# Thirteen pairs of value pieces as 2x2 block products of seven instead of eight, in the second half of both value stages

## The reference, cut to what matters

```python
def block(args):
    ht, et, gt = args
    act = jax.nn.gelu(jnp.einsum('td,ted->te', ht, u[et]), approximate=False)
    return jnp.einsum('te,ted->td', gt * act, v[et])
```

## Time and profile before

| | us |
|---|---|
| median of three runs | 2201.44 (2199.56 to 2203.94) |
| span of the profiled execution | 2200.3 |
| TensorE busy | 2187.5 (99%) |
| VectorE busy | 1649.6 (75%) |
| ScalarE busy | 1223.3 (56%) |
| GpSimd busy | 719.4 (33%) |

### The profile page before, as it was taken

One profiled execution on the slowest core, in us unless ns is written; L12 is line 12 of the kernel. 1 busy time (PEld: TensorE's weight loads), 2 busy tenths in 40 slices (PEclk: granted clock), 3 DMA queues, 4 the chain that ended last, 5 costly groups with the idle time before them and its releaser, 6 DMA issues.

```text
span 2200.3 us, 43642 instructions
## 1 busy us (share of the span) xinstructions
PE 2187.5 (99%) x14230; PEld 1905.3 (87%) x14230; DVE 1649.6 (75%) x3276; ACT 1223.3 (56%) x1933; POOL 719.4 (33%) x737
## 2 busy tenths in 40 slices
PE   9999999999999999999999999999999999999999
PEld 8899888888888888888988888888888888899887
DVE  8776885888888755666678678888886556558895
ACT  6555555555544445565565555554444446566764
POOL 1506886333344100002088853324440001530000
PEclk9999999999999999999999999999999999999999
DMA  5265665555655566554556655555556665545665
GB/s 175 97 200 156 189 188 176 172 172 170 187 177 179 180 193 191 172 192 134 173 172 186 188 180 173 172 167 187 174 179 193 203 194 172 163 141 159 187 190 162
DMA packets 109819, 385.88 MB, mean 175 GB/s; under 512 B 12545, under 2 KB 15009, under 8 KB 109473
## 3 DMA queue, kind: packets, MB, share of 16 engines
q1 hardware_dynamic: 106864, 382.34, 55.8%
q10 hardware_dynamic: 2864, 2.36, 0.3%
HBM read 383.46 MB, written 1.06 MB: 175 GB/s over the span
## 4 chain that ended last, share of the span: by engine, by line
PE 92%; DVE 5%; POOL 1%; DMA 1%; ACT 1%; issue 1%; SPq 0%; ACTq 0%; DVEq 0%; POOLq 0%
PE bank L2395 24%; PE bank L2367 13%; PE bank L2447 11%; PE bank L2449 11%; PE bank L2448 11%; PE bank L2283 3%; PE bank L2271 3%; PE bank L2275 3%; PE bank L2807 3%; PE bank L2590 1%; DVE w_lo L1259 1%; POOL big L506 1%; PE bank L2491 1%; PE bank L2492 1%; PE bank L2493 1%; PE bank L2775 1%
## 5 line engine op out<-in xcount | busy, mean ns | idle before, releaser
L583 ACT ACTIVATE w_hi<-ring 128x1024 fp32r<-128x1024 f32 x699 | 738.1, 1057 | 509.5 <-PE bank L2449 362.9
L1259 DVE TENSOR_TENSOR w_lo<-ring,w_hi 128x1024 fp32r<-128x1024 f32 x548 | 670.3, 1225 | 261.7 <-ACT w_hi L583 261.7
L2395 PE MATMUL bank<-x_parts,w_hi 128*128 128x512 f32 x2320 | 583.1, 393 | 0.3 <-ACT w_hi L583 0.3
L2395 PEld LDWEIGHTS bank<-x_parts,w_hi 128*128 128x128 f32 x2320 | 416.9, 189 | 75.0 <-issue 0.4
L467 POOL TENSOR_TENSOR w_lo<-ring,w_hi 128x1024 fp32r<-128x1024 f32 x151 | 364.2, 2418 | 266.0 <-DVE x_parts L1244 160.4
L2447 PE MATMUL bank<-w_hi,x_parts 128*128 128x512 f32 x1024 | 400.8, 391 | 0.0
L2449 PE MATMUL bank<-w_lo,x_parts 128*128 128x512 f32 x1024 | 398.7, 389 | 0.0
L2448 PE MATMUL bank<-w_hi,x_parts 128*128 128x512 f32 x1024 | 398.3, 389 | 0.0
L479 POOL COPY quads<-sco 128x32 f16 (+1 forms) x256 | 226.2, 912 | 445.7 <-DVE sco L1751 445.6
L2367 PEld LDWEIGHTS bank<-x_parts,w_lo 128*128 128x128 f32 x2368 | 324.3, 190 | 25.0 <-DVE w_lo L1259 2.9
L2367 PE MATMUL bank<-x_parts,w_lo 128*128 128x256 f32 x2368 | 335.7, 283 | 0.2 <-DVE w_lo L1259 0.2
(11 more groups left out here) (368 smaller groups left out, 2747.9 us busy)
## 6 DMA issues: line engine op xcount, KB each, us to landing
ring<-u_dram SPq DMA_DIRECT2D x256, 512.0 KB, 3.6
ring<-v_dram SPq DMA_DIRECT2D x256, 512.0 KB, 4.1
ring<-up_dram SPq DMA_DIRECT2D x44, 512.0 KB, 4.2
ring<-wq_dram SPq DMA_DIRECT2D x32, 512.0 KB, 4.2
ring<-sb_in_dram SPq DMA_DIRECT2D x31, 512.0 KB, 3.9
ring<-od_in_dram SPq DMA_DIRECT2D x25, 512.0 KB, 4.0
ring<-down_dram SPq DMA_DIRECT2D x22, 512.0 KB, 4.3
ring<-ev_in_dram SPq DMA_DIRECT2D x21, 512.0 KB, 3.7
```

The costliest lines, as they stand in the source:

```text
L583: A(w_hi[:, k % RING, :], ring[:, k % RING, :], ACT.Copy).then_inc(g["w_hi_done"], 1)
L1259: V.tensor_tensor(w_lo[:, k % RING, :], ring[:, k % RING, :], w_hi[:, k % RING, :].bitcast(F32), ALU.subtract).then_inc(g["lo_dve"], 1)
L2395: mm(dst[:, :], hi[:, rows[c]], x_both[:, c, :], start=(c == 0), stop=False, skip_group_check=True)
```

## The change

In the second half of a value stage, 26 of the 64 pieces are taken as 13 pairs. A pair is two pieces and their activations: a 2x2 block matrix of activations (two token blocks by two pieces) times a 2x2 block matrix of weights (two pieces by two column blocks of `CB = 512`). The plain way needs eight block products; the change uses the scheme of seven products, with four sums of weight blocks (`weight_sums`, 1024, 512 and 512 columns in three GpSimd instructions) and four sums of activation blocks (`act_sums`, four GpSimd instructions of 128 columns). Each of the seven products is three matmuls, so a pair takes 21 instead of 24. The products go to seven banks, and the blocks that belong to several outputs are added up once at the end (`pair_ends`).

The order on TensorE is four plain pieces (`HEAD`), then thirteen times a pair and two plain pieces (`BETWEEN`), then eight plain ones (`TAIL`): 38 plain pieces (`DIRECT`) and 13 pairs. The pair's weights don't go through the ring: `load_pair` brings them into two buffers in `big`, and ScalarE and VectorE make their high and low parts in four instructions each (`pair_part`, parts 0 to 3: 1536, 2048, 512 and 384 columns). Pairs 0 and 1 are loaded in the middle of the first half, and GpSimd's sums of pair 0 stand between its last table copies there. The core of the diff:

```diff
+HEAD, COUPLED, BETWEEN, TAIL = 4, 13, 2, 8
+DIRECT = HEAD + COUPLED * BETWEEN + TAIL
...
+            def load_pair(layer, s):
+                k, raw = couple_row(s), pair_raw[s % 2]
+                for at, row in ((0, k + 1), (PIECE, k)):
+                    sp.dma_start(raw[:, at:at + PIECE], a[f"v{layer}"][row]).then_inc(pair_loaded[s % 2], 16)
...
+            def first_pairs(layer):
+                sp.wait_ge(g["pieces_used"], starts[f"v{layer}"] + 16)
+                load_pair(layer, 0)
+                load_pair(layer, 1)
...
+                for d in range(DIRECT):
+                    s = pair_after(d - 1)
+                    s = s + 2 if s is not None else 0
+                    if 2 <= s < COUPLED:
+                        sp.wait_ge(*weights_summed(layer, s - 2))
+                        sp.wait_ge(*pair_low(layer, 4 * (s - 2) + 1))
+                        load_pair(layer, s)
+                    sp.wait_ge(*low_bits(k0 + d - RING))
+                    load(a[f"v{layer}"][direct_row(d)], k0 + d)
...
+            def weight_sums(layer, s):
+                raw, out = pair_raw[s % 2], pair_sum[s % 3]
+                if s >= 3:
+                    pool.wait_ge(*pair_free(layer, s - 3))
...
+                pool.wait_ge(*pair_arrived(layer, s))
...
+                pool.tensor_tensor(b3(out[:, 0:2 * CB], 2), b12, b3(raw[:, CB:3 * CB], 2), ALU.subtract).then_inc(g["pair_summed"], 1)
+                pool.wait_ge(*weights_summed(layer, s, 1))
+                pool.tensor_tensor(out[:, 2 * CB:3 * CB], raw[:, CB:2 * CB], out[:, CB:2 * CB], ALU.subtract).then_inc(g["pair_summed"], 1)
+                pool.wait_ge(*weights_summed(layer, s, 2))
+                pool.tensor_tensor(out[:, 3 * CB:4 * CB], raw[:, 0:CB], out[:, 2 * CB:3 * CB], ALU.subtract).then_inc(g["pair_summed"], 1)
...
+                for d in range(DIRECT):
+                    direct_chunk(d)
+                    if d == HEAD - 2:
+                        pair_part(0, 2)
+                        pair_part(0, 3)
+                    s = pair_after(d)
+                    if s:
+                        for part in range(4):
+                            pair_part(s, part)
...
+                    dve.wait_ge(*pair_high(layer, 4 * s + part + 1))
+                    dst, src, high = ((pair_lo[b], pair_raw[b][:, 0:3 * CB], pair_hi[b][0]), (pair_sum_low[s % 3], pair_sum[s % 3], pair_hi[b][1]),
+                                      (low_acts, acts, act_hi[b][:, 0:4 * P]), (act_sum_low[b], act_sum[b], act_hi[b][:, 4 * P:7 * P]))[part]
+                    V.tensor_tensor(dst, src, high.bitcast(F32), ALU.subtract).then_inc(g["pair_low"], 1)
...
+            def accumulate_coupled(layer):
...
+                for d in range(DIRECT):
+                    direct(d)
+                    s = pair_after(d)
+                    if s is not None:
+                        couple(s)
...
-                accumulate(HALF)
+                accumulate_coupled(layer)
```

More of the change, by code:

```diff
@@ L82, in build @@
         bank = [ctx.enter_context(nc.psum_tensor(f"bank{i}", [P, 512], F32)) for i in range(8)]
+        with nc.sbuf_tensor("below_sums", [P, 8 * CB], F32), nc.sbuf_tensor("sums_low", [P, 8 * CB], F32R) as sums_low, \
+                nc.sbuf_tensor("parts", [P, 16 * CB], F32R) as parts:
+            pass
+        with nc.sbuf_tensor("below_acts", [P, 64 * T], F32), nc.sbuf_tensor("acts_low", [P, 64 * T], F32R) as acts_low:
+            pass
         big = sb("big", [P, 128 * T])
@@ L88, in build @@
         xT = sb("xT", [P, KC * T])
+        with nc.sbuf_tensor("x_plain", [P, KC * 2 * T], F32) as x_plain:
+            pass
         x_parts = sb("x_parts", [P, KC * 2 * T], F32R)
+        with nc.sbuf_tensor("sco_rounded", [P, TB * 16 * NK], F32R) as sco_rounded:
+            pass
         sco = sb("sco", [P, TB * 16 * NK])
@@ L257, in build @@
         x_quarter = [sem(f"x_quarter{i}") for i in range(4)]
+        pair_loaded = [sem(f"pair_loaded{i}") for i in range(2)]
         POOL, DVE, WHOLE = range(3)
@@ L307, in released_before, with pair_arrived, pair_free, pair_high @@
             return 3 * (k - 1) + (1, 1, 4, 4, 7)[k - 1]
+        def pair_arrived(layer, s):
+            return pair_loaded[s % 2], 32 * (layer * ((COUPLED + 1 - s % 2) // 2) + s // 2 + 1)
+        def pair_free(layer, s, half=2):
+            return g["pair_used"], (2 * COUPLED + 3) * layer + 2 * s + half
+        def pair_high(layer, count):
+            return g["pair_high"], (4 * COUPLED + 1) * layer + count
+        def pair_low(layer, count):
+            return g["pair_low"], (4 * COUPLED + 4) * layer + count
+        def weights_summed(layer, s, count=3):
+            return g["pair_summed"], 7 * COUPLED * layer + (0, 3)[s] + count if s < 2 else 7 * (COUPLED * layer + s) + count
+        def acts_summed(layer, s, count=4):
+            return g["pair_summed"], 7 * COUPLED * layer + (6, 10)[s] + count if s < 2 else 7 * (COUPLED * layer + s) + 3 + count
         def unit_bank(u):
@@ L519, in _ @@
                             quadruple(layer, groups * half + 3 + q, i)
+                    if half:
+                        weight_sums(layer, 0)
                     for m in range(3 + 3 * loops, groups):
                         quadruple(layer, groups * half + m)
+                weight_sums(layer, 1)
+                act_sums(layer, 0)
+                act_sums(layer, 1)
+                for s in range(2, COUPLED):
+                    weight_sums(layer, s)
+                    act_sums(layer, s)
                 if layer == 0:
@@ new lines, in experts @@
+                e11, e12, e21, e22 = (pair_ends[:, j * CB:(j + 1) * CB] for j in range(4))
+                for d in range(DIRECT):
+                    direct(d)
+                    if d == 0:
+                        pair_part(0, 0)
+                    if d == 1:
+                        pair_part(0, 1)
+                    if d == HEAD - 2:
+                        pair_part(0, 2)
+                        pair_part(0, 3)
+                    s = pair_after(d)
+                    if s:
+                        for part in range(4):
+                            pair_part(s, part)
+                    if d == DIRECT - 3:
+                        dve.wait_ge(*pair_high(layer, 4 * COUPLED + 1))
+                        step(V.tensor_tensor(e21, bank[2][:, :], e11, ALU.add))
+                        settle()
+                        step(V.tensor_tensor(e12, bank[1][:, :], e21, ALU.add))
+                    if d == DIRECT - 2:
+                        settle()
+                        step(V.tensor_tensor(e22, bank[3][:, :], e12, ALU.add))
+                        step(V.tensor_tensor(e21, bank[3][:, :], e21, ALU.add))
@@ L1835, in _ @@
+                settle()
+                for j in range(4):
+                    if j < 3:
+                        dve.wait_ge(*pair_free(layer, COUPLED, j + 1))
+                    else:
+                        dve.wait_ge(g["pieces_used"], k0 + DIRECT - 1)
+                    V.tensor_tensor(bank[4 + j][:, :], bank[4 + j][:, :], pair_ends[:, j * CB:(j + 1) * CB], ALU.add).then_inc(g["pair_low"], 1)
+                ax[0] += DIRECT
+                residual(HALF + DIRECT, False)
             experts(0)
```

214 lines of the change are left out of this document (161 added, 53 removed).

## The result

The changed kernel takes 2290.48 us (median of four runs, 2288.44 to 2293.39), the kernel before 2201.38 in the same session (2199.56 to 2203.94): ratio 1.0408, 95% interval 1.0394 to 1.0423. It is 89 us slower; the forecast was 87.

A forecast was written before the change was run, and what follows sets the result against it. TensorE was taken to bound the kernel before. Per layer, +40 us in the second half and 3.5 at the first half's end: 2 x (40 + 3.5) = 87 us on the median of 2201.4 gives 2288 us, range 2245 to 2325.

The forecast's parts named there:

- What TensorE saves: Second half of a value stage: 21 matmuls for 24 in each of 13 pairs save 8.8 us a layer, 17.7 in all.
- First reason, the loop: SyncE's queue: next pair's loads wait for VectorE's part 0, so landing and splitting follow in series, 12.6 us a cycle.
- The landing of 1.5 MB: Three 512 KB loads issued together by SyncE, a pair's and the next plain piece's, land in 6.5 us (5.7 to 7.6).
- Second reason, the turns: GpSimd's sums and VectorE's subtractions exclude each other: 14.6 us a cycle in all; two half sums add 2.5 in the loop.
- Small sums as hidden: GpSimd's four 128-column sums fall partly where VectorE waits before part 0: counted as nothing, up to 1.7 us if not.
- The cycle: A pair and two plain pieces in the second half: 12.6 + 2.5 = 15.1 us, bounds 14.2 and 17.
- The sum: Ten cycles of 15.1 us against TensorE's 10.2, less 8.8 saved: +40 us a layer.
- End of the first half: GpSimd's sums among its last table copies and the loads of pairs 0 and 1 cost 3.5 us a layer (0.5 to 8).
- the lead of 2.8: Lead of about 2.8 us of the other engines over TensorE at the start, set against first work on pairs.
- Loop but no mutual blocking: Rival: in the second half GpSimd's sums happen to lie in VectorE's gaps; +11 us a layer, 2224 us, chance 8%.
- TensorE stays the bound: Rival: loads land in 5.0 us and GpSimd's sums block nothing in the second half; 2184 us in full, chance 4%.
- The clock falls: Rival: TensorE's clock falls to 1.2 GHz in the new waits, cycle 20.4 us, about 2390 us, chance 5%.

The follow-up runs named there:

- run 3: Changed kernel with pair loads two plain pieces later in SyncE's queue and GpSimd's sums 8 columns wide (sums left out of the computation): 2182.55 us, ratio 0.9919.
- run 2: Changed kernel with GpSimd's seven sums of a pair 8 columns wide (sums left out of the computation), queue unchanged: 2227.86 us, ratio 1.0132.
- run 1: Changed kernel with each pair's loads issued two plain pieces later in SyncE's queue: 2262.12 us, ratio 1.0278.
- run 4: Kernel before, with GpSimd's seven subtractions of a pair added thirteen times in each second half on unused data: 2217.78 us, ratio 1.0079.
- run 5: Changed kernel with the sums of pairs 0 and 1 after the table copies and ScalarE's part 1 of pair 0 one plain piece later: 2302.69 us.
- run 6: Changed kernel with seven pairs, five plain pieces between, loads two pieces later, sums of pairs 0 and 1 after the table copies, still on GpSimd: 2216.08 us.
- run 7: Changed kernel with seven pairs, five plain pieces between, loads two pieces later, first GpSimd sums around the table copies as in the change: 2206.95 us.
- run 10: Changed kernel with seven pairs, four plain pieces between, six ahead, all sums on VectorE, loads two pieces later, pair 0's parts one piece later: 2257.96 us.
- run 9: Changed kernel with its 13 pairs and two plain pieces between, all sums on VectorE, loads two pieces later: 2214.38 us, ratio 1.0067.

## Why the prediction was right, step by step

- **What TensorE saves**, 8.8 us a layer: run 3 shows it nearly whole (8.4 in the stage of layer 0).
- **First reason, the loop.** Forecast 12.6 us; alone it is 12.8 in the mean (run 2). The landing of 1.5 MB, taken as 6.5 between bounds of 5.7 and 7.6, was 6.8 from the first issue to ScalarE's start. The burst of the earlier trace rows came nearer to it. The estimate of 5.6 by the Trainium skill (DMA: Bandwidth & Descriptors, "Anatomy of one DMA — SWDGE (gpsimd) path"), a fit for the path of GpSimd's loads and not of SyncE's, is 1.2 us short. Run 1 shows that without the loop the change is 28 us faster.
- **Second reason, the turns.** Forecast: 14.6 us of work that must go one after the other, 2.5 of it inside the loop. Run 1 has 13.8 for the first, the change has 5.04 + 2.01 for 2.98 + 1.75 in the loop, 2.3 for the second. As the earlier trace rows showed, the later instruction waits for the whole of the other: 0.42 us became 2.62 beside a sum of 2.41 (run 4). The Trainium skill (SBUF — State Buffer, "Who interferes with whom") has it that the later one of two such instructions blocks fully, and the runs agree but for the ends. The overlap at the ends, which I took from the earlier trace rows for the lower bound only, is there at each change of turns and was worth 0.8 us a cycle in run 1; that sum should have had it.
- **Small sums as hidden**: wrong. Three of four fell in the loop, at 0.25 us each, 0.8 together. The two half sums, counted at 2.5, cost only 1.5 there, since the first had begun 0.7 us before VectorE. That the whole comes to 2.3 for 2.5 is partly luck. GpSimd's own time for the seven was 10.5 us from first to last, since each turn costs it a VectorE instruction.
- **The cycle**, 15.1: measured 15.05 and 14.91. Both reasons were off by some tenths in opposite directions.
- **The sum.** 10 x (15.0 - 10.2) - 8.8 = +39 a layer. End of the first half: +3.5 forecast, 2.04 and 1.77 us of waits measured in layer 0, before L2659 and L3066 (2.2 us in layer 1), with a 0.42 us instruction at 2.62 and a 1.23 one at 3.29 beside GpSimd's sums. So 43 of the 45.6 are the forecast's. The missing 2.6 lie, as far as the waits show, at the start of the second half, where I had let the lead of 2.8 pay for the first work on pairs. TensorE's timeline of the changed kernel has both places:

```profile
731.89 0.47 PE L2659 MATMUL bank<-w_hi,x_parts 128*128 128x512 f32 x1 [2.04 <-DVE x_parts L1431]
...
737.58 0.64 PE L3066 MATMUL bank<-sco 128*128 128x64 f16 x16 [1.77 <-DVE sco L1916]
...
756.99 0.47 PE L2702 MATMUL bank<-w_hi,x_parts 128*128 128x512 f32 x1 [1.19 <-DVE x_parts L1431]
...
763.90 0.47 PE L2702 MATMUL bank<-w_hi,x_parts 128*128 128x512 f32 x1 [3.91 <-DVE x_parts L1431]
```

Run 3 gives the measure. From the stage's first matmul to part 0 of pair 1 the changed kernel takes 211.4 us and run 3 201.8, 9.6 less; behind part 0 of pair 11 the changed kernel takes 4.1 less than run 3, the lead that it has used up by then. So the start costs 5.5 us where the forecast had 3.5. No run separates in it the end of the first half from the first work on pairs, and run 5 shows that the waits of the two do not simply add up.
- **The last additions**: nothing, as said.
- **Rivals.** *Loop but no mutual blocking* had 2224; run 2, which makes just this true, took 2227.9. *TensorE stays the bound* had 2184; run 3 took 2182.6. *The clock falls* was half right: it falls to 1.2 GHz, but for some 3 us of 15 in part of the cycles (0.89 in the mean), not for good, and costs nothing there, as TensorE does not set the cycle. Its place was elsewhere: where a wait is followed by work that TensorE bounds (runs 6 and 7) or whose end the others wait for (run 10).

## What to carry to other kernels

- An engine that is idle is not free. Before work goes to GpSimd beside VectorE with both operands in SBUF, add both engines' times as if they were one engine's; here the same sums cost 80 us on the idle GpSimd, and half as many pairs with them on the busy VectorE were a gain.
- A load that waits for work of this cycle, with the next cycle's load behind it in the queue, puts its whole landing time in a loop; move it behind those loads.
- Fewer matmuls on the bound are worth just their time, but only if the others keep up in each cycle and at its start. Compare the chain from the release of a ring slot to the last part with the pieces that the ring holds, not busy shares: in run 10 VectorE had time to spare, and TensorE waited 3.2 us a cycle.

## What the runs showed of the hardware that was not expected

- TensorE's granted clock did not stay at 1.00 with waits, nor fall for good. With 1.0 us of wait in each cycle of 11.5 us (run 9) it was 1.00; with 3.2 us in each of about 20 (run 10) it was 0.93; with two waits of 0.8 to 2.8 in 15 (the changed kernel) 0.89 or 1.00 by turns; behind waits of 3.83 and 2.24 us (run 6) 0.66 and 0.83 for ten microseconds each. Two waits of the same length at the same place can differ: behind 2.04 us at 731.89 in the changed kernel it stayed at 1.00, behind 2.03 us at 735.25 in run 7 it fell to 0.50 for some three us. What that costs depends on what follows: nothing where VectorE ends the next wait anyway (the changed kernel, and the first stretch of run 6), 1.4 to 1.8 us for each fall where TensorE's own end counts (runs 6, 7 and 10).
- Turns between GpSimd and VectorE are taken by instruction, whatever their size: a 0.42 us instruction took 2.62 us. Whether splitting GpSimd's work in smaller pieces helps was not tried.
